# Gathering the second expert table by four tokens and two heads, and multiplying it in four 32-column groups

## The chip, the cores and the metric

The kernel runs on one core of a Trainium2 chip. The metric is the device time of one execution in microseconds (us): the median of 3 runs of the kernel before is 1951.93 us (1950.73 to 1953.85). Lower is better.

## The reference

One decoder layer over 512 tokens of width 1024: an attention part, a gated DeltaNet part, an output projection, and then a retrieval layer over 128 x 128 experts (PEER). Only the last one is touched:

```python
s1, s2 = query halves @ keys1, keys2           # 8 heads x 128 keys each, per token
v1, i1 = top_k(s1, 16); v2, i2 = top_k(s2, 16)
top_score, pos = top_k(v1[..., :, None] + v2[..., None, :], 16)
expert_id = (i1 * 128 + i2)[pos]; gate = softmax(top_score)
# per token 8 heads x 16 = 128 selections
act = gelu(einsum('tkd,td->tk', u_tab[expert_id], h))
y = einsum('tk,tkd->td', gate * act, v_tab[expert_id])
x = x + y
```

Each of the 512 tokens reads 128 rows of `peer_u` and 128 rows of `peer_v`, all of 1024 float32 (4 KB): 131,072 rows, 537 MB.

## The kernel before

Up to the output projection everything is unrolled; the PEER layer then works on 4 tiles of 128 tokens, one token in each partition. For a tile there are 128 steps c (head h = c // 16, rank k = c % 16). All of it meets in these steps:

- GpSimd (`gather`, L456 to L488) issues for each c one indirect DMA of 128 rows of `peer_u` (row p is the expert that token p chose as its selection c) into one of 8 buffers `u_row`, and one of `peer_v` into one of 8 buffers `v_row`. `peer_v` runs one head (16 steps) behind `peer_u`. In the first tile `peer_v` is held until head 2 and is then issued twice per step for 16 steps. Both kinds are in one instruction stream: a gather that waits for its buffer holds back those behind it.
- VectorE (`tile`, L1320 to L1360) waits for the u row and multiplies and sums it against h in one instruction (L1336), which frees the u buffer. After each head it waits for ScalarE's gelu and makes the weights `wt` (L1355). Between steps it also runs `choose` (L1273), the top-k of one head: in the first tile its own heads at c in `FIRST_AT`, and for the next tile the eight heads at c = 88, 93, ..., 123 (`NEXT_AT` and every 5). The next tile's ids go to `eid_n` and are copied into `eid` by `take` (L1313) when the gathers have read the old ones.
- ScalarE (`diagonal`, L945) turns each column of weights into a 128 x 128 diagonal matrix, in one of 8 buffers.
- TensorE (L763 to L791) multiplies the diagonal by the v row in two halves of 512 columns, which adds the weighted rows of 128 tokens to PSUM banks 6 and 7. After it the v buffer is free. Between these it computes the next tile's queries: half a query with every step from c = 36 to 67 (L736), then 16 score matmuls (L744) at c = 68.
- When a tile is done, ScalarE's `finish` copies the banks to `y_s`, and SyncE stores it.

The four tiles are written as tile 0, a hardware loop over tiles 1 and 2, and tile 3 (`tiles`, L281). Waits on buffers whose number depends on the loop go through `by_itself` (L276), which adds an increment of a semaphore behind the wait.

## Time and profile before

| | before |
|---|---|
| median of 3 runs | 1951.93 us |
| lowest, highest | 1950.73, 1953.85 us |
| the profiled execution, its span | 2155.2 us |
| granted TensorE clock, mean | 0.912 |
| bytes moved by the gathers (software queue) | 536.94 MB |
| DMA engines' share, whole span | 66.9% in the gathers |

Times of instructions come from one profiled execution. It is 203 us longer than the median. The first gather is issued 522.6 us into it, the last at 2140.1 us. In rows of a timeline the columns are start in us, length in us, engine, line, operation, and in brackets how long the engine was idle before it and for whom. "issue" means that nothing in the profile shows what it waited for. The diagram of 40 slices shows the PEER layer from slice 10 on:

```profile
PEclk9999999889896998888989877899998879999999
DMA  3212020142696898889999977999997889999997
```

### The profile page before, as it was taken

How to read it: one execution, taken by the hardware profiler on the slowest of the kernel's cores; microseconds unless marked ns; L12 is line 12 of the kernel's file. 1: busy time of each engine (PE TensorE's matmuls, PEld its weight loads, DVE VectorE, ACT ScalarE, POOL GpSimd, SP SyncE). 2: the span in 40 equal slices, each digit the busy share in tenths (PEclk: the TensorE clock that was granted, in tenths of full speed). 3: DMA queues.
4: the chain of work that ended last, by engine and by line, in shares of the span. 5: the costliest groups of instructions: out<-in, count | busy, mean ns of one | idle time of the engine just before them, and what ended most of it. 6: DMA issues, size and time to landing. Idle time of an engine off the chain costs nothing.

```text
span 2155.2 us, 19891 instructions
## 1 busy us (share of the span) xinstructions
PE 1638.5 (76%) x5306; PEld 838.8 (39%) x5306; DVE 1147.4 (53%) x2739; ACT 346.6 (16%) x780; POOL 1046.2 (49%) x1111
## 2 busy tenths in 40 slices
PE   5989989888782977567769765686895567676778
PEld 3445567767331543223236422232552222222223
DVE  3424446564857436884454477545436784444441
ACT  2331223221120111111111111211111111111111
POOL 3001012202463565566666555666665566666664
PEclk9999999889896998888989877899998879999999
DMA  3212020142696898889999977999997889999997
GB/s 119 78 39 79 0 78 1 40 147 94 247 359 239 330 346 314 294 303 364 379 345 337 336 276 288 359 378 349 351 350 297 301 301 365 374 375 348 366 368 290
DMA packets 161218, 571.36 MB, mean 265 GB/s; under 512 B 19152, under 2 KB 19152, under 8 KB 160080
## 3 DMA queue, kind: packets, MB, share of 16 engines
q0 software_dynamic: 147456, 536.94, 66.9%
q1 hardware_dynamic: 13648, 33.10, 4.3%
q8 instruction: 47, 0.77, 0.1%
q14 instruction: 67, 0.55, 0.1%
HBM read 567.87 MB, written 2.10 MB: 264 GB/s over the span
## 4 chain that ended last, share of the span: by engine, by line
PE 40%; issue 19%; DVE 18%; DMA 7%; POOL 7%; DVEq 5%; another core or an unknown queue 2%; ACT 1%; POOLq 1%; ACTq 0%
PE psum L788 15%; DVE arena L1336 7%; POOL arena L458 6%; PE psum L538 5%; PE psum L736 4%; PE psum L536 4%; DMA arena<-in_peer_u,arena 4%; DMA arena<-in_peer_v,arena 3%; DVE arena L1245 2%; PE psum L590 1%; DVE arena L1246 1%; PE psum L650 1%; DVE arena L1242 1%; DVE arena L1249 1%
## 5 line engine op out<-in xcount | busy, mean ns | idle before, releaser
L788 PE MATMUL psum<-arena 128*128 128x512 f32 x2048 | 1014.9, 634 | 352.8 <-DMA arena<-in_peer_v,arena 138.3
L1336 DVE CUSTOM_DVE_ANT_0 arena<-arena,psum 128x1024 f32<-128x1024 f32 x512 | 613.5, 1220 | 516.4 <-DMA arena<-in_peer_u,arena 413.9
L788 PEld LDWEIGHTS psum<-arena 128*128 128x128 f32 x2048 | 385.1, 201 | 910.9 <-issue 848.0
L458 POOL DMA_INDIRECT arena<-in_peer_u,arena x512 | 482.6, 943 | 381.6 <-issue 211.2
L458 POOL DMA_INDIRECT arena<-in_peer_v,arena x512 | 484.2, 946 | 340.0 <-issue 138.9
L948 ACT ACTIVATE arena<-ident,arena 128x128 f32<-128x128 f32 x512 | 175.5, 393 | 605.2 <-PE psum L788 328.1
L422 POOL TENSOR_TENSOR arena<-arena 128x512 f32<-128x512 f32 x28 | 37.1, 1335 | 249.2 <-DVE arena L1176 135.8
L736 PEld LDWEIGHTS psum<-arena 128*128 128x128 f32 x1024 | 132.4, 194 | 63.5 <-issue 63.5
L736 PE MATMUL psum<-arena 128*128 128x128 f32 x1024 | 135.3, 278 | 13.2 <-issue 11.7
L538 PE MATMUL psum<-arena 128*128 128x512 f32 x256 | 114.0, 592 | 0.0
L980 ACT ACTIVATE arena<-arena 128x16 f32<-128x16 f32 x32 | 6.9, 217 | 519.1 <-DVEq L1346 380.9
L536 PE MATMUL psum<-arena 128*128 128x512 f32 x192 | 86.5, 606 | 0.0
L538 PEld LDWEIGHTS psum<-arena 128*128 128x128 f32 x256 | 46.7, 190 | 49.3 <-issue 49.3
L713 PE MATMUL psum<-arena 128*128 128x512 f32 x128 | 57.3, 608 | 1.4 <-ACT arena L926 1.4
L436 POOL TENSOR_TENSOR arena<-arena,g_rs 128x512 f32<-128x512 f32 x8 | 9.1, 1174 | 99.0 <-DVEq L1119 99.0
L536 PEld LDWEIGHTS psum<-arena 128*128 128x128 f32 x192 | 36.7, 195 | 42.7 <-issue 42.4
L1249 DVE MAX8 arena<-arena 128x8 f32<-128x128 f32 (+1 forms) x96 | 29.3, 333 | 27.5 <-issue 23.8
L1336 DVE DVE_READ_ACCUMULATOR2_ANT arena<- 128x1 f32 x512 | 42.2, 82 | 0.0
L730 PE MATMUL psum<-ident,arena 128*128 128x128 f32 x32 | 6.9, 386 | 45.0 <-DVE arena L1266 45.0
L744 PE MATMUL psum<-arena 128*128 128x128 f32 x128 | 22.1, 350 | 24.0 <-ACT arena L937 17.7
L661 PE MATMUL psum<-arena 128*128 128x128 f32 x192 | 38.6, 296 | 0.0
L660 PE MATMUL psum<-arena 128*128 128x128 f32 x160 | 35.7, 308 | 3.8 <-ACT arena L909 3.7
(197 smaller groups left out, 1241.7 us busy)
## 6 DMA issues: line engine op xcount, KB each, us to landing
arena<-in_w_in SPq DMA_DIRECT2D x7, 2048.0 KB, 8.4
arena<-in_peer_w_q SPq DMA_DIRECT2D x8, 1024.0 KB, 5.9
arena<-in_peer_u,arena POOLq DMA_INDIRECT x512
arena<-in_peer_v,arena POOLq DMA_INDIRECT x512
arena<-in_w_out SPq DMA_DIRECT2D x8, 512.0 KB, 7.0
arena<-in_x SPq DMA_DIRECT2D x4, 512.0 KB, 4.7
out<-arena SPq DMA_DIRECT2D x4, 512.0 KB
arena<-in_norm_g SPq DMA_DIRECT2D x1, 512.0 KB, 4.1
```

What stands on the lines that cost most here:

```text
L422: pool.tensor_tensor(ATs[n % 2], AT, lv_mask[:, lv].unsqueeze(1).to_broadcast([P, GH, P]), ALU.mult).then_inc(s["ats_rdy"], 1)
L458: pool.indirect_dma_start(buf, None, table, bass.IndirectOffsetOnAxis(ap=eid[:, col:col + 1], axis=0)).then_inc(landed, 16)
L536: mm = pe.matmul(ps, w[:, dc, u * P:(u + 1) * P], hT[:, dc], start=dc == 0, stop=dc == DC - 1)
L538: mm = pe.matmul(ps, hT[:, dc, u * P:(u + 1) * P], w[:, dc], start=dc == 0, stop=dc == DC - 1)
L661: mm = pe.matmul(bank[6][:, c], XW[:, h], tt, start=True, stop=True)
L713: mm = pe.matmul(bank[wo_bank(n)], mixT[:, t, c], w_out_s[c][:, half * 512:(half + 1) * 512], start=c == 0, stop=c == DC - 1)
L736: mm = pe.matmul(bank[j // 4][:, (j % 4) * P:(j % 4 + 1) * P], w_q_s[c][:, j * HALF:(j + 1) * HALF], h2T[:, c], start=c == 0, stop=c == DC ...
L788: mm = pe.matmul(bank[6 + half], diag[c % VB], v_row[c % VB][:, half * 512:(half + 1) * 512], start=False, stop=c == SEL - 1, skip_group_c ...
L948: act.activation(diag[c % VB], ident[:], ACT.Copy, scale=wt[:, c:c + 1]).then_inc(s["diag_rdy"], 1)
L1245: dve.max_index(i_[:, 0:8], o[:, 0:8], v)
L1249: dve.max(o[:, 8:16], l_)
L1336: dve.tensor_tensor_reduce(u_row[c % UB], u_row[c % UB], h2p, 1.0, 0.0, ALU.mult, ALU.add, dots[:, c:c + 1]).then_inc(s["u_free"], 1)
```

## The change

It changes what one gather of `peer_v` holds. Before, it holds one selection of 128 tokens. Now it holds 32 selections (two heads, a "unit") of 4 tokens. The product with the weights then sums over the partitions, so that TensorE needs a 128 x 4 matrix of weights in place of a diagonal one. That matrix is 32 columns wide (28 of them zero), it writes 32 partitions of PSUM, and four gathers in a row go to the four groups of 32 columns. The parts:

- `choose` transposes the ids of each two heads in blocks of 32 x 32 on VectorE (`eidT`). `weigh` does so for the weights, and spreads them with one multiplication into `zrows` (two of them, in turn), where each gather's four columns stand in a window of 32. ScalarE's 512 diagonals are gone.
- TensorE's `rows` takes four gathers at a time: 8 matmuls, and one increment of `v_free` by 4 behind them. Buffers of v are freed four at a time. The number of matmuls and the columns that they stream are as before.
- `peer_v` runs a unit (32 steps) behind `peer_u`, never two to a step. After the last u gather, 32 v gathers are left, where 16 were.
- `eid` and `gates` have two buffers each; `take` is gone. The gelu is one for each unit (16 in all, not 32), and VectorE makes the weights one step into the next unit, so it doesn't wait for it on the spot.
- The tiles are written out, without the loop and without `by_itself`.
- Places: the next tile's chooses stand at c = 100, 103, ..., 121 in tile 0 and at 72, 77, ..., 107 in tiles 1 and 2 (before 88, 93, ..., 123 in all). The queries stand at c = 66 to 81, two halves a step, in tile 0, and at 22 to 53 in tiles 1 and 2; scores at 82 and 54.
- The result goes in place into `xs`, in an order of tokens that `swap` (a permuted identity) sets, and is stored with four DMAs a tile.

The diff, cut:

```diff
+UH = 2
+UK = UH * TOPK
+NQ = P // UK
+UNITS = NT * PH // UH
+ZG, ZW = 36, 32
...
-        FIRST_AT = [3, 22, 35, 38, 41, 44, 47]
+        FIRST_AT = [3, 19, 35, 38, 41, 44, 47]
...
+                self.norm = 47 if i == 0 else 15
+                self.turn = 2 * UK if i == 0 else 20
+                self.query = self.turn + 2
+                self.step = 2 if i == 0 else 1
+                self.score = self.query + 2 * NS // self.step
+                self.choose = 100 if i == 0 else 72
+                self.every = 3 if i == 0 else 5
...
+        def unit_rows(j):
+            group, place = j % NQ, j // NQ
+            return group, place, group * (UK // NQ) + place
...
-            with sp.Fori(0, NT) as i:
-                sp.wait_ge(s["y_out"], i + 2)
-                sp.dma_start(out_d[:, bass.ds(i, 1)].rearrange("p o d -> p (o d)"), y_s).then_inc(s["stored"], 16)
+            for i in range(NT):
+                sp.wait_ge(s["y_out"], i + 1)
+                for q in range(NQ):
+                    sp.dma_start(out_d[q * UK:(q + 1) * UK, i], xs[q::NQ, i]).then_inc(s["stored"], 16)
...
+            def gather_v(k, j):
+                n = k * UK + j
+                at_ = unit_rows(j)[2]
+                if j == 0:
+                    pool.wait_ge(s["eidT_rdy"], k + 1)
+                if n >= VB:
+                    pool.wait_ge(s["v_free"], n - VB + 1)
+                pool.indirect_dma_start(v_row[n % VB], None, v_d,
+                                        bass.IndirectOffsetOnAxis(ap=eidT[k % (2 * PH // UH)][:, at_:at_ + 1], axis=0)
+                                        ).then_inc(v_in[n % VB], 16)
...
+            for i in range(NT):
+                for c in range(SEL):
+                    k, j = divmod(i * SEL + c, UK)
+                    gather_u(i, c)
+                    if k == 1 and j == 0:
                         pool.wait_ge(s["wo_ps"], 2 * NT)
-                        if is_first(i) and h <= 2:
-
-                            if h == 2:
-                                gather_v(0, 2 * k)
-                                gather_v(0, 2 * k + 1)
-                        elif h >= 1:
-                            gather_v(i * SEL, (h - 1) * TOPK + k)
+                        pool.memset(zrows[0], 0.0)
+                        pool.memset(zrows[1], 0.0).then_inc(s["z_clear"], 1)
+                    if k >= 1:
+                        gather_v(k - 1, j)
+            for j in range(UK):
+                gather_v(UNITS - 1, j)
...
+                    pe.wait_ge(s["z_rdy"], k + 1)
+                last = k % (SEL // UK) == SEL // UK - 1 and j + NQ == UK
                 for half in range(2):
+                    for jj in range(j, j + NQ):
+                        n = k * UK + jj
+                        group, place, at_ = unit_rows(jj)
+                        z0 = at_ * ZG - place * (ZG - ZW)
+                        if half == 0:
+                            pe.wait_ge(v_in[n % VB], 16 * (n // VB + 1))
+                        mm = pe.matmul(bank[6 + half][group * UK:(group + 1) * UK],
+                                       zrows[k % 2][:, z0:z0 + ZW],
+                                       v_row[n % VB][:, half * 512:(half + 1) * 512],
+                                       start=False, stop=last, skip_group_check=True)
+                mm.then_inc(s["v_free"], NQ)
...
-                    pe.wait_ge(s["diag_rdy"], i * SEL + c + 1)
-                    pe.wait_ge(v_in[c % VB], 16 * (i * (SEL // VB) + c // VB + 1))
-                    for half in range(2):
-                        mm = pe.matmul(bank[6 + half], diag[c % VB], v_row[c % VB][:, half * 512:(half + 1) * 512],
-                                       start=False, stop=c == SEL - 1, skip_group_check=True)
-                    mm.then_inc(s["v_free"], 1)
...
-            def diagonal(row, c):
-                act.wait_ge(s["v_free"], SEL + row + c - VB + 1)
-                act.activation(diag[c % VB], ident[:], ACT.Copy, scale=wt[:, c:c + 1]).then_inc(s["diag_rdy"], 1)
...
+                if h % UH == UH - 1:
+                    k = (t * PH + h) // UH
+                    if k >= 2 * PH // UH:
+                        dve.wait_ge(s["v_free"], (k - 2 * PH // UH + 1) * UK)
+                    dve.drain()
+                    dve.transpose(eidT[k % (2 * PH // UH)], into_id[:, (h - UH + 1) * TOPK:(h + 1) * TOPK]).then_inc(s["eidT_rdy"], 1)
...
+            def weigh(k):
+                i = k * UK // SEL
+                c = slice(k * UK % SEL, k * UK % SEL + UK)
+                dve.wait_ge(s["gel_rdy"], k + 1)
+                dve.drain()
+                dve.tensor_tensor(wt[:, c], gel[:, c], gates[i % 2][:, c], ALU.mult)
+                dve.drain()
+                dve.transpose(wT, wt[:, c])
...
+                dve.drain()
+                dve.tensor_tensor(zrows[k % 2].rearrange("p (g x) -> p g x", x=ZG)[:, :, 0:NQ].rearrange("p (a b) x -> p a b x", a=NQ),
+                                  wT.rearrange("p (a b) -> p a b", a=NQ).unsqueeze(3).to_broadcast([P, NQ, UK // NQ, NQ]),
+                                  quarter.unsqueeze(1).unsqueeze(1).to_broadcast([P, NQ, UK // NQ, NQ]),
+                                  ALU.mult).then_inc(s["z_rdy"], 1)
...
+                    if c % UK == 1 and n >= UK:
+                        weigh(n // UK - 1)
+            weigh(UNITS - 1)
```

## Rows read from the trace of the kernel before

**Rows 1.** The page: the span, and busy time by engine (us, share, instructions).

```profile
span 2155.2 us, 19891 instructions
PE 1638.5 (76%) x5306; PEld 838.8 (39%) x5306; DVE 1147.4 (53%) x2739; ACT 346.6 (16%) x780; POOL 1046.2 (49%) x1111
```

**Rows 2.** Windows: stretch, length, each engine's busy us, granted clock, DMA share, GB/s.

```profile
600.00:700.00 100.00, 56.55 (x127) 22.83 (x126) 67.32 (x226) 9.83 (x26) 50.45 (x54) 0.83 0.79 293
700.00:800.00 100.00, 92.87 (x399) 56.13 (x398) 44.14 (x77) 14.87 (x40) 61.76 (x66) 0.99 0.91 332
800.00:950.00 150.00, 92.47 (x210) 40.13 (x209) 110.28 (x358) 20.32 (x50) 80.74 (x86) 0.84 0.84 309
1200.00:1350.00 150.00, 94.59 (x212) 42.85 (x211) 108.25 (x352) 18.32 (x48) 79.62 (x85) 0.79 0.81 295
1600.00:1750.00 150.00, 94.03 (x230) 40.90 (x229) 104.68 (x332) 18.12 (x47) 79.10 (x83) 0.85 0.80 293
1800.00:2100.00 300.00, 213.19 (x424) 74.62 (x423) 129.99 (x219) 40.71 (x120) 196.09 (x209) 0.97 0.96 368
```

**Rows 3.** The gathers' line L458: what ended GpSimd's idle time before them.

```profile
  DVE arena L1336: 168.3, 57
  PE psum L788: 156.4, 63
```

**Rows 4.** Timeline of GpSimd, tile 0; the second row is step c = 80.

```profile
772.74 0.94 POOL L458 DMA_INDIRECT arena<-in_peer_v,arena  x1 [3.35 <-remote]
773.99 0.94 POOL L458 DMA_INDIRECT arena<-in_peer_u,arena  x1 [0.30 <-DVE arena L1336]
```

**Rows 5.** Timeline of VectorE, tile 3: two u rows one after the other.

```profile
2107.79 1.22 DVE L1336 CUSTOM_DVE_ANT_0 arena<-arena,psum 128x1024 f32<-128x1024 f32 x1 [1.33 <-DMA arena<-in_peer_u,arena]
2110.35 1.22 DVE L1336 CUSTOM_DVE_ANT_0 arena<-arena,psum 128x1024 f32<-128x1024 f32 x1 [1.33 <-DMA arena<-in_peer_u,arena]
```

**Rows 6.** Timeline of VectorE: a choose from first to last instruction, then two u rows.

```profile
813.96 0.50 DVE L1242 MAX8 arena<-psum 128x8 f32<-128x128 f32 x2 [9.01 <-PE psum L744]
...
823.04 0.17 DVE L1297 SCALAR_TENSOR_TENSOR arena<-arena 128x16 uint32<-128x16 f32 x1
823.22 1.22 DVE L1336 CUSTOM_DVE_ANT_0 arena<-arena,psum 128x1024 f32<-128x1024 f32 x1
...
824.37 1.22 DVE L1336 CUSTOM_DVE_ANT_0 arena<-arena,psum 128x1024 f32<-128x1024 f32 x1
```

**Rows 7.** Timeline of VectorE: first and last instruction of a later choose.

```profile
644.67 0.50 DVE L1242 MAX8 arena<-psum 128x8 f32<-128x128 f32 x2
...
662.17 0.18 DVE L1297 SCALAR_TENSOR_TENSOR arena<-arena 128x16 uint32<-128x16 f32 x1
```

**Rows 8.** Timeline of GpSimd: step 32 of tile 0, the first v rows behind it.

```profile
585.75 0.94 POOL L458 DMA_INDIRECT arena<-in_peer_u,arena  x1 [1.11 <-issue]
587.00 0.94 POOL L458 DMA_INDIRECT arena<-in_peer_v,arena  x1 [0.30 <-DVE arena L1336]
```

**Rows 9.** Timeline: the last u gather, the last gelu, the last products.

```profile
2110.68 0.94 POOL L458 DMA_INDIRECT arena<-in_peer_u,arena  x1 [0.30 <-issue]
...
2119.73 0.21 ACT L980 ACTIVATE arena<-arena 128x16 f32<-128x16 f32 x1 [15.26 <-DVEq L1346]
...
2126.63 24.27 PE L788 MATMUL psum<-arena 128*128 128x512 f32 x56 [0.56 <-issue]
```

**Rows 10.** Timeline of TensorE: one step's query half, one v row; tile 0's scores.

```profile
798.07 1.05 PE L736 MATMUL psum<-arena 128*128 128x128 f32 x8
...
798.96 1.88 PE L788 MATMUL psum<-arena 128*128 128x512 f32 x4
...
808.25 5.52 PE L744 MATMUL psum<-arena 128*128 128x128 f32 x32 [7.42 <-ACT arena L937]
```

**Rows 11.** Timeline of VectorE: a head's end inside the choose stretch of tile 0.

```profile
899.65 0.08 DVE L1336 DVE_READ_ACCUMULATOR2_ANT arena<- 128x1 f32 x1
900.29 0.18 DVE L1355 TENSOR_TENSOR arena<-arena 128x16 f32<-128x16 f32 x1 [0.56 <-ACT arena L980]
```

More of the change, by code:

```diff
@@ L486, in _, with gather_u @@
-            pool.wait_ge(s["mixT_ps"], NT)
-            tiles(pool, tile)
-            for k in range(TOPK):
-                gather_v((NT - 1) * SEL, (PH - 1) * TOPK + k)
+            def gather_u(i, c):
+                n = i * SEL + c
+                if c % TOPK == 0:
+                    pool.wait_ge(s["eid_rdy"], i * PH + c // TOPK + 1)
+                if n >= UB:
+                    pool.wait_ge(s["u_free"], n - UB + 1)
+                pool.indirect_dma_start(u_row[n % UB], None, u_d, bass.IndirectOffsetOnAxis(ap=eid[i % 2][:, c:c + 1], axis=0)
+                                        ).then_inc(u_in[n % UB], 16)
@@ L771, in tile @@
+            for i in range(NT):
                 for c in range(SEL):
-                    if not is_last(i):
-                        if c == TURN_AT:
+                    w = PLACES[i]
+                    if i + 1 < NT:
+                        if c == w.turn:
                             pe.wait_ge(s["picked"], (i + 1) * PH)
                             turn_h2(i + 1)
-                        if QUERY_AT <= c < SCORE_AT:
-                            if c == QUERY_AT:
+                        if w.query <= c < w.score:
+                            if c == w.query:
@@ L779, in tile @@
                                 pe.wait_ge(s["h2T_out"], i + 2)
-                            mm = query((c - QUERY_AT) // 2, (c - QUERY_AT) % 2, 2)
-                            if c == SCORE_AT - 1:
+                            for x in range((c - w.query) * w.step, (c - w.query + 1) * w.step):
+                                mm = query(x // 2, x % 2, 2)
+                            if c == w.score - 1:
                                 mm.then_inc(s["q_ps"], 1)
-                        if c == SCORE_AT:
+                        if c == w.score:
@@ L795, in _ @@
+                    if k >= 1 and j % NQ == 0:
+                        rows(k - 1, j)
+            for j in range(0, UK, NQ):
+                rows(UNITS - 1, j)
         @block.scalar
@@ L966, in load_h2, with gelu @@
                 ins.then_inc(s["h2p_rdy"], 1)
+            def gelu(k):
+                c = slice(k % (SEL // UK) * UK, (k % (SEL // UK) + 1) * UK)
+                act.wait_ge(s["dots_rdy"], k + 1)
+                act.activation(gel[:, c], dots[:, c], ACT.Gelu).then_inc(s["gel_rdy"], 1)
             turned_h2(0)
@@ L1255, in norm2 @@
             def norm2(t):
-                xt = x2[:, bass.ds(t * D, D)]
-                if not is_first(t):
-                    by_itself(dve, s["h2T_ps"], t)
+                xt = xs[:, t]
+                if t:
+                    dve.wait_ge(s["h2T_ps"], t)
                 dve.drain()
@@ L1362, in _ @@
-            tiles(dve, tile)
+                choose(0, h, h == EARLY - 1)
+            soften(0, gates[0], 0, EARLY)
+            for i in range(NT):
+                dve.wait_ge(s["h2p_rdy"], i + 1)
+                for c in range(SEL):
+                    n = i * SEL + c
+                    if i == 0 and c in RESIDUAL_AT:
+                        residual(3 + RESIDUAL_AT.index(c))
+                    dve.wait_ge(u_in[n % UB], 16 * (n // UB + 1))
+                    dve.tensor_tensor_reduce(u_row[n % UB], u_row[n % UB], h2p, 1.0, 0.0, ALU.mult, ALU.add,
+                                             dots[:, c:c + 1]).then_inc(s["u_free"], 1)
+                    if c % UK == UK - 1:
+                        dve.drain()
+                        dve.engine_nop().then_inc(s["dots_rdy"], 1)
+                    if c == PLACES[i].norm and i + 1 < NT:
+                        norm2(i + 1)
+                    if chosen_after(i, c):
+                        who, head = chosen_after(i, c)
+                        last = head in ([PH - 1] if who else [h1 - 1 for _, h1, _ in GROUPS0])
+                        choose(i + who, head, last)
+                    for group, (h0, h1, after) in enumerate(GROUPS0):
+                        if i == 0 and c == after:
+                            soften(group, gates[0], h0, h1)
+                    if i >= 1 and c == SOFTEN_AT:
+                        soften(len(GROUPS0) + i - 1, gates[i % 2], 0, PH)
+                    if c % UK == 1 and n >= UK:
+                        weigh(n // UK - 1)
```

220 lines of the change are left out of this document (77 added, 143 removed).

## The prediction

> **What bounds the kernel now.** I read the busy times first, then the layer in windows, then what ends the waits of the gathers, and last the timelines from which the prices come. The totals show no full engine: VectorE is busy 53% and GpSimd 49% of a span of 2155.2 us [rows 1]. The windows tell more. In tile 3, where nothing but rows is worked on, the DMA engines are at a share of 0.96 and move 368 GB/s [rows 2]: transfers are the bound there. In the three stretches in which the next tile's heads are chosen the share falls to 0.84, 0.81 and 0.80, while VectorE is busy 110, 108 and 105 of 150 us [rows 2]: there VectorE is the bound. In the stretch with the queries TensorE is busy 93 of 100 us, and the share is 0.91 [rows 2]: there TensorE takes part. The waits of the gathers say the same twice: 168 us until VectorE has freed a u buffer, 156 us until TensorE has freed a v buffer [rows 3]. Part of this is harmless, since GpSimd issues a gather every 1.25 us (773.99 less 772.74) [rows 4], and the transfers are slower than that: two u rows, between which lie two gathers, follow each other by 2.56 us (2110.35 less 2107.79) [rows 5], 1.28 us a gather. At that pace 1024 gathers take 1311 us.
>
> The number of gathers, their bytes and the streamed columns of TensorE stay. So the change can only win or lose the time in which the transfers stand still. Over the six windows of rows 2 that is, with (1 less share) by length, 21, 9, 24, 29, 30 and 12 us.
>
> **Profile and median.** The profiled execution is 203 us longer than the median, and no row tells in which stretch. I sum changes against the span of 2155.2 us and carry the sum to the median unscaled, since its terms are made of VectorE's and TensorE's instruction times and of the 2.56 us a pair, the quickest steady pace seen.
>
> **The places of the chooses.** One choose takes 9.26 us from its first to its last instruction (823.22 less 813.96), and a u row costs 1.15 us of VectorE when rows are waiting (824.37 less 823.22) [rows 6]. From c = 88 to 128, tile 0 needs VectorE before for 40 x 1.15 + 8 x 9.26 = 120 us, against 40 x 2.56 = 102 us of transfers. After, c = 88 to 100 goes at the transfers' pace (12 x 2.56 = 31 us), then 28 x 1.15 + 74 = 106 us on VectorE: 137 us. The denser places cost 17 us in tile 0. Some chooses take longer in the profile (17.7 us, 644.67 to 662.35, with gaps that nothing explains) [rows 7]. The difference of the two cases does not depend on it, since both have eight of them. In tiles 1 and 2 the spacing is 5 as before: 0.
>
> **What VectorE no longer waits for.** A head's end costs it 0.8 us inside such a stretch (899.65 to the weights at 900.29, and 0.18 for them) [rows 11], three times a stretch, and `take`, its wait, and the switch to the next tile fall into it too, some 2 us. In tiles 1 and 2 the stretch now ends at c = 107, and there is one `weigh` in it. I give the new transposes and `weigh` 1.5 us a unit, worked out as a handful of small instructions like the 0.18 us one of rows 11 with their drains. The trace has none of them: bounds 0.5 and 4 us a unit. Gain about 3 us in each of the three stretches: 9 us less, bounds 0 and 15.
>
> **The v gathers that come later.** Before, 16 v gathers are fitted in two behind each u gather, at c = 32 to 47 of tile 0, from 587.0 on [rows 8]. There VectorE has five chooses and 16 rows, 5 x 9.26 + 16 x 1.15 = 65 us, and 48 gathers need 61 us: they were nearly free. After, only 32 are there, 41 us, and the transfers stand. The 16 lie at the end. There before, from the issue of the last u gather at 2110.7 [rows 9] to the end of the span 44.5 us pass: the last gelu at 2119.7, the last 14 v rows on TensorE in 24.27 us (56 records, four a row) [rows 9], 1.73 us each, then copies and the store. After: gelu as before, weights 2 us later, a first group of four rows, then 24 gathers at 1.28 to 1.44 us (31 to 35), the last group, copies, four stores: some 58 us if the four column groups run side by side, and 9 + 2 + 32 x 1.73 + 5 = 71 us if they don't. That is 13 to 27 us more. The early part gives 5 us back: step 35, and with it the row of chooses that bounds this part, comes sooner when one gather goes with each step and not two. Sum 8 to 22 us, 10 taken with side by side.
>
> **TensorE.** An undisturbed v row costs 1.88 us, half a query 1.05, the scores 5.5 us and before them 7.4 us of waiting for ScalarE's copy [rows 10]. Before, a step with a query costs 2.9 us against 2.56: over 32 steps 12 us behind, then 13 us for the scores. Eight v buffers cover 8 x 2.56 = 20 us of it, so some 5 us a tile are lost, 15 in all. After, four steps cost 4.2 us of queries and the rows of a group, which lies between 1.9 (all side by side) and 7.5 us (none), against 10.2. In tiles 1 and 2 that is no loss in most of this range. In tile 0 the queries come two halves a step: 8.4 us and the rows, 10.3 to 15.9, against 10.2, over four groups, and then the scores. The loss stays there. Gain 10 us; with no overlap of the groups 0, and even a loss of 3.
>
> What shows TensorE's speed is the granted clock: 0.97 in tile 3 and 0.79 to 0.85 where it starves between rows [rows 2], between full speed (2.4 GHz) and half (1.2 GHz). Catching up after such a stretch gets cheaper with groups: 4 us less.
>
> **Buffers freed in fours.** The worst gather of v must now wait until the group five rows back is done, not until one row eight back is. When it waits, four v and about five u gathers are still under way: 9 x 1.28 = 11.5 us of transfers. TensorE's work behind the last landed row of a group is at most five rows' halves at 0.94, 4.7 us at full clock and 9.4 at half; issue and first data take another 3 us (I take the 2.56 us of rows 5 and round up). It fits but for half the clock. 0, bounds 0 and 15 us.
>
> **Removed at no gain.** The 512 diagonals lie beside the gathers' bound. The increments behind the waits lie beside as well: step 80 begins a head and so has two waits with increments ahead of its gather, and the gap before it is 0.30 us [rows 4], the same as elsewhere. The loop's end likewise. The two memsets on GpSimd (some 2 us, ahead of the first v gather; everything behind them in its queue waits) lie in a part that VectorE bounds.
>
> **The sum.** +17 - 9 + 10 - 10 - 4 = +4 with the groups fully side by side. With none it is +17 - 9 + 22 + 3 = +33. The pairs of records of one float32 matmul go to the same columns one behind the other, so I expect half the overlap, and take +14: 2169 us of span, 1966 us of median.
>
> The Trainium skill, "TensorE: Matmul & The Clock Gate" (Part 3, packing small matmuls), gives a speedup of 2.38 for three column tiles of 32 with 512 columns, and says that matmuls keep their order in start and end. No row here shows a column tile. By it the sum would lie at the lower end, near +6.
>
> **The rivals.**
> *TensorE holds the gathers, and the change frees them.* For it: 156 us of waits for v buffers [rows 3], 92.87 of 100 us busy [rows 2]. Against it: where TensorE is fullest the transfers lose only 9 us in 100. If the median runs, with quicker transfers than the profile, are held by TensorE in the query and catching-up stretches, then 3 x (9 + 5) = 42 us come from there (the 9 us of that window and 5 us of lag, for each of three tiles). With the 9 us of VectorE and less the 17 of tile 0 that is 34 less: 1918 to 1940. Chance 0.28.
> *Nothing moves.* Transfers are the bound, and gains and losses cancel within 4 us: 1952. For it speaks the sum for full overlap. The skill's "DMA: Bandwidth & Descriptors" (Specifications) puts a core's share of HBM at about 358 GB/s, by which the layer would be bound by transfers wherever it is placed. Tile 3 moves 368 GB/s over 300 us [rows 2], above it. Chance 0.12.
> *The groups don't overlap and come late.* This ends slower by more: the worst case of the sum, 33, and half a clock in the gaps between groups, which makes up to 15 us: 1985 to 2000. It decides when the rows of a group take over 8.5 us behind the last landing (11.5 less 3). Chance 0.15.
> *The forecast*, 1958 to 1983: 0.45. If the new instructions ask for another order of time altogether (a store by rows of four partitions, say), that is outside all of these.
>
> **How the numbers follow.** The likeliest is 1966. Faster cases hold 0.28, so the range reaches down to 1925, and up to 2005 with most of the third case. A measurement of this kernel tells 0.2%, 4 us, from no change. Slower by more than that: 0.45 + 0.15 = 0.60, within 0.12, faster 0.28.
>
> **What would show it.** In the profile after: in c = 100 to 127 of tile 0 the DMA share under 0.7 with VectorE nearly full, and waits on L1336 there. From the last u gather to the end 55 to 70 us, not 44.5. Shares of 0.95 or more where the queries are in tiles 1 and 2. If groups overlap, the products' busy time falls well under 1000 us. Waits for TensorE's v buffers under 100 us say that the relief is real. I'm wrong if tile 0 and the tail are longer by less than 15 us together, or if tile 3 alone gets quicker or slower than 2.56 to 2.9 us a pair.

## The result, and the profile after

The changed kernel takes 1972.88 us (median of 4 runs, 1967.81 to 1975.73) against 1951.33 us for the kernel before on the same chip: a ratio of 1.0111, interval 1.0089 to 1.0134. It is 21.6 us slower, where 14 us slower was forecast.

Chips differ. On some, here called quick, the kernel before takes about 1951 us; on others, called slow, 2124 to 2156. (Three chips were slow, and the one of c3, e6b and e7 was quick; that of this first comparison isn't on record. No chip was met twice, so it isn't shown that a chip always keeps its pace.) The trace that the prediction read is from a slow one, and the trace of after from a quick one. So the rows of before that answer to it are those of a later run of the kernel before on a quick chip (c3_before_third, below), and ratios are always of two kernels on one chip. Where rows 1 have a span of 2155.2 us and rows 3 waits of 168.3 and 156.4 us, the page and the view of the gathers' line of before say this on a quick chip:

```profile
span 1955.1 us, 19891 instructions
PE 1601.5 (82%) x5306; PEld 822.5 (42%) x5306; DVE 1148.1 (59%) x2739; ACT 353.1 (18%) x780; POOL 1042.3 (53%) x1111
DMA  3121120014279899999999999999999999999997
L458 POOL DMA_INDIRECT arena<-in_peer_u,arena x512: 932/937/1548, 525.4 to 1903.5; - x171
  DVE arena L1336: 106.8, 109
  PE psum L788: 85.9, 124
```

And after (L475 is now the u gather, L486 the v gather, L795 the product, L1313 the copy that ends a choose):

```profile
span 1966.0 us, 16121 instructions
PE 1378.3 (70%) x5306; PEld 548.1 (28%) x5306; DVE 1151.7 (59%) x2765; ACT 166.8 (8%) x250; POOL 1047.4 (53%) x1116
DMA  3121120023379799979999979999997999999998
L795 PE MATMUL psum<-arena 128*32 128x512 f32 x2048 | 754.2, 825 | 507.3 <-DMA arena<-in_peer_v,arena 416.7
L475 POOL DMA_INDIRECT arena<-in_peer_u,arena x512: 932/937/1835, 516.8 to 1898.9; - x171
  DVE arena L1365: 125.9, 100
L486 POOL DMA_INDIRECT arena<-in_peer_v,arena x512: 932/937/1843, 579.8 to 1952.9; - x171
  PE psum L795: 74.9, 54
DMA to landing us min/median/max: 4.9/9.0/11.8
```

The diagrams of 40 slices, counted from 0, tell a part. On a quick chip before has 9s from slice 14 to the last but one; after has 7s between them, in the stretches in which the next tile's heads are chosen (slices 17, 23, 30), as at 13, where the first tile's own are. But a 9 is 90% or anything above. The page's row of GB/s, of before and then of after, shows that before's choose stretches fall too, to between 334 and 375 (slices 17, 23 to 25, 30 to 32), only less deep than after's:

```profile
GB/s 131 54 76 43 44 86 1 1 49 156 68 278 394 316 396 396 380 334 372 410 409 407 390 375 336 351 410 409 408 409 373 351 337 410 409 410 409 409 409 282
GB/s 130 53 76 43 44 86 1 6 81 118 129 278 356 261 409 409 339 249 366 410 409 409 398 288 410 410 409 409 409 401 282 410 409 409 410 410 409 409 376 297
```

TensorE lost 223 us of busy time and ScalarE half of its own, and the span is no shorter. From the first u gather to the end it is 1955.1 less 525.4 = 1429.7 us before and 1966.0 less 516.8 = 1449.2 after: 19.5 us longer. (The part ahead of it varies by several us between runs of one program and isn't touched.)

Windows on quick chips show where. Before: steps 32 to 63, 64 to 95 and 96 to 127 of tile 0 by the issues of their u gathers, then tile 3, then from the last u gather on (stretch, length, busy of PE, PEld, DVE, ACT, POOL, clock, DMA share, GB/s):

```profile
584.00:699.00 115.00, 86.76 (x226) 38.99 (x227) 90.26 (x269) 21.77 (x54) 75.42 (x80) 0.90 0.91 354
699.00:783.00 84.00, 83.76 (x374) 51.86 (x373) 44.52 (x99) 13.51 (x35) 59.68 (x64) 1.00 1.02 400
783.00:880.00 97.00, 68.78 (x144) 27.95 (x142) 88.72 (x282) 12.63 (x34) 60.71 (x66) 0.88 0.95 357
1582.00:1903.00 321.00, 241.61 (x493) 86.17 (x494) 165.06 (x301) 50.83 (x143) 237.74 (x254) 0.98 1.02 404
1903.00:1955.00 52.00, 42.68 (x96) 17.28 (x94) 8.78 (x15) 6.94 (x19) 16.95 (x19) 1.00 0.75 290
```

After, the same stretches:

```profile
574.00:684.00 110.00, 54.59 (x127) 8.60 (x125) 92.33 (x276) 3.06 (x4) 62.91 (x66) 0.71 0.81 298
684.00:764.00 80.00, 66.60 (x420) 39.25 (x421) 37.98 (x66) 3.11 (x3) 59.67 (x64) 0.89 1.03 409
764.00:876.00 112.00, 66.69 (x140) 8.83 (x135) 93.95 (x311) 1.51 (x2) 60.28 (x65) 0.64 0.85 316
1571.00:1899.00 328.00, 209.01 (x511) 30.38 (x508) 159.66 (x269) 4.38 (x9) 238.34 (x256) 0.75 1.03 409
1899.00:1966.00 67.00, 46.94 (x154) 7.96 (x154) 5.61 (x11) 1.30 (x3) 31.68 (x34) 0.91 0.82 303
```

Counted by the u rows as VectorE takes them up (the starts of the instruction that the prediction has at L1336, now L1365): steps 0 to 63 of tile 0 are 7.3 us shorter (177.9 to 170.6), 64 to 87 the same, 88 to 127 12.4 longer (127.7 to 140.1: the dense chooses), tile 1 is 12.5 shorter (353.1 to 340.6), tile 2 2.8 shorter, tile 3 6.2 longer, and from the last u row to the end 35.0 us have become 58.1. Together +19.5. Tiles 2 and 3 belong together: before leaves tile 2 with VectorE behind and catches up in tile 3 (its first 16 u rows there take 35.9 us, and 16 rows of the steady part 41.0 in both kernels).

### The profile page after: what moved, and what is told of

Read it like the earlier page. It is cut to its first block, busy times and chain, and to the rows that moved or that the text cites. A ratio compares the mean times of both kernels' runs of the same rounds, so it can differ in the third digit from the quotient of the medians.

```text
span 1966.0 us, 16121 instructions
## 1 busy us (share of the span) xinstructions
PE 1378.3 (70%) x5306; PEld 548.1 (28%) x5306; DVE 1151.7 (59%) x2765; ACT 166.8 (8%) x250; POOL 1047.4 (53%) x1116
## 4 chain that ended last, share of the span: by engine, by line
PE 25%; DVE 23%; DMA 20%; POOL 17%; issue 9%; DVEq 4%; ACT 1%; POOLq 0%; ACTq 0%
DMA arena<-in_peer_u,arena 11%; DVE arena L1365 10%; DMA arena<-in_peer_v,arena 9%; POOL arena L486 8%; POOL arena L475 8%; PE psum L551 6%; PE psum L549 4%; PE psum L795 3%; DVE arena L1260 2%; PE psum L726 2%; PE psum L603 2%; DVE arena L1261 1%; PE psum L663 1%; DVE arena L1257 1%; DVE arena L1264 1%
## 5 line engine op out<-in xcount | busy, mean ns | idle before, releaser
L795 PE MATMUL psum<-arena 128*32 128x512 f32 x2048 | 754.2, 825 | 507.3 <-DMA arena<-in_peer_v,arena 416.7
L1365 DVE CUSTOM_DVE_ANT_0 arena<-arena,psum 128x1024 f32<-128x1024 f32 x512 | 613.8, 1218 | 439.5 <-DMA arena<-in_peer_u,arena 437.8
L475 POOL DMA_INDIRECT arena<-in_peer_u,arena x512 | 482.4, 942 | 322.0 <-DVE arena L1365 125.9
L486 POOL DMA_INDIRECT arena<-in_peer_v,arena x512 | 482.0, 941 | 217.0 <-issue 141.0
L795 PEld LDWEIGHTS psum<-arena 128*32 128x32 f32 x2048 | 113.2, 127 | 1122.7 <-DMA arena<-in_peer_v,arena 875.7
L749 PEld LDWEIGHTS psum<-arena 128*128 128x128 f32 x1024 | 117.3, 193 | 25.6 <-issue 25.6
L749 PE MATMUL psum<-arena 128*128 128x128 f32 x1024 | 121.9, 279 | 1.2 <-ACT arena L962 1.2
L551 PE MATMUL psum<-arena 128*128 128x512 f32 x256 | 114.0, 592 | 0.0
L549 PE MATMUL psum<-arena 128*128 128x512 f32 x192 | 85.8, 602 | 0.0
L726 PE MATMUL psum<-arena 128*128 128x512 f32 x128 | 63.3, 656 | 9.2 <-DVE arena L1244 7.7
L551 PEld LDWEIGHTS psum<-arena 128*128 128x128 f32 x256 | 46.7, 190 | 49.3 <-issue 49.3
L549 PEld LDWEIGHTS psum<-arena 128*128 128x128 f32 x192 | 36.3, 193 | 42.2 <-issue 42.0
L1365 DVE DVE_READ_ACCUMULATOR2_ANT arena<- 128x1 f32 x512 | 42.2, 83 | 0.0
L726 PEld LDWEIGHTS psum<-arena 128*128 128x128 f32 x128 | 26.5, 211 | 44.0 <-issue 44.0
L674 PE MATMUL psum<-arena 128*128 128x128 f32 x192 | 37.6, 289 | 0.0
L1084 DVE TENSOR_SCALAR arena<-arena,cwc 128x512 f32<-128x512 f32 x12 | 6.7, 561 | 52.3 <-ACT arena L865 52.1
L673 PE MATMUL psum<-arena 128*128 128x128 f32 x160 | 34.6, 301 | 3.9 <-ACT arena L938 3.7
L663 PE MATMUL psum<-arena 128*128 128x128 f32 x192 | 26.4, 280 | 8.6 <-DVE arena L1222 6.1
```

The source lines that it names most:

```text
L475: pool.indirect_dma_start(u_row[n % UB], None, u_d, bass.IndirectOffsetOnAxis(ap=eid[i % 2][:, c:c + 1], axis=0)).then_inc(u_in[n % UB], 16)
L486: pool.indirect_dma_start(v_row[n % VB], None, v_d, bass.IndirectOffsetOnAxis(ap=eidT[k % (2 * PH // UH)][:, at_:at_ + 1], axis=0)).then_i ...
L549: mm = pe.matmul(ps, w[:, dc, u * P:(u + 1) * P], hT[:, dc], start=dc == 0, stop=dc == DC - 1)
L551: mm = pe.matmul(ps, hT[:, dc, u * P:(u + 1) * P], w[:, dc], start=dc == 0, stop=dc == DC - 1)
L663: mm = pe.matmul(bank[4][:, h * P:(h + 1) * P], ATs[n % 2][:, h], TI[:, h] if i else ident[:], start=True, stop=True)
L726: mm = pe.matmul(bank[wo_bank(n)], mixT[:, t, c], w_out_s[c][:, half * 512:(half + 1) * 512], start=c == 0, stop=c == DC - 1)
```

## Experiments

All spaced kernels change constants of the list of places alone. They were made to say which part of the change costs what, in the changed kernel.

**The kernel before again**, unchanged, one execution.

> The kernel before, unchanged, for a second trace. The profile of the kernel after has a span of 1966.0 us, that is its own measured time, its gathers follow each other at 1.28 us and every choose takes 9.2 to 9.6 us. The first profile of before has a span of 2155.2 us, 203 us over its median, a pair of gathers every 2.8 us in tile 3 and chooses of up to 21 us. Theory: that one execution was a disturbed one, and a second trace shows a span of 1945 to 1960 us, 2.56 us a pair in tile 3 and chooses of 9.3 us. Rival: the kernel before is slowed whenever it is profiled (its hardware loop or its many small instructions), and the span is again 2100 us or more.

2123.72 us, on a slow chip, where eleven other executions of the kernel before took 2127 to 2143 us. So the 203 us between the first trace and the median are no cost of the profile.

**The chooses of tile 0 at their old spacing.**

```diff
-                self.choose = 100 if i == 0 else 72
-                self.every = 3 if i == 0 else 5
+                self.choose = 88 if i == 0 else 72
+                self.every = 5
```

> The kernel after with the chooses of tile 0 at c = 88, 93, ..., 123 in place of 100, 103, ..., 121, as the kernel before has them. Theory (the prediction's first term): the dense places cost 12 x (2.56 - 1.15) = 17 us, so this runs 17 us (12 to 20) faster than after's 1972.9, near 1956. Rival 1: eight buffers of u rows cover the lag in both, and it is within 4 us of after. Rival 2: a wait of the unit's weights behind the lagging chooses (the products of a new unit start at c = 97) takes back half of it, gain 5 to 10 us.

0.9875 (0.9847 to 0.9902) of before on a slow chip.

**The chooses of tiles 1 and 2 over more steps.**

```diff
-                self.choose = 100 if i == 0 else 72
-                self.every = 3 if i == 0 else 5
+                self.choose = 100 if i == 0 else 60
+                self.every = 3 if i == 0 else 8
```

> The kernel after with the chooses of tiles 1 and 2 at c = 60, 68, ..., 116 in place of 72, 77, ..., 107. In the trace of after, c = 64 to 111 takes 141 us in tile 1 where a stretch without chooses takes 123, so 18 us are lost in each. With a choose in every 8 steps VectorE needs 8 x 1.15 + 9.3 = 18.5 us against 20.5 us of transfers and never falls behind. Theory: both losses go, 30 to 36 us faster than after, near 1940, and faster than before. Rival: the transfers stand for another reason there (v buffers freed in fours, the scores on TensorE), and it is within 6 us of after.

0.9816 (0.9786 to 0.9845), slow chip.

**Both.** `self.choose = 88 if i == 0 else 60`, `self.every = 5 if i == 0 else 8`.

> The places of both: tile 0 at 88 and every 5, tiles 1 and 2 at 60 and every 8. Theory: the gains add, 45 to 55 us faster than after, near 1923, 1.5% faster than before. Rival: the gains overlap, since one slack covers both, and it is no faster than the better of the two by over 5 us.

0.9754 (0.9726 to 0.9782), slow chip.

**The changed kernel again**, since the three before it had run on another chip than it, and **the kernel before again**.

> The kernel after, unchanged. The job before this one ran on a chip on which the kernel before takes 2136 us, not 1951, and a pair of gathers 2.8 us, not 2.56. On such a chip the transfers leave VectorE more time in the choose stretches. If the gains of the two changes of places add, after took 2107.6 + 2095.4 - 2082.7 = 2120 us there, 0.993 of before. Theory: on a slow chip after is at 0.990 to 0.997 of before, on a quick one (before at 1951) at 1.011 again. Rival: the change costs the same everywhere, and the ratio is 1.008 or more on a slow chip too; then the two changes of places did not add, and each was worth over 40 us.

> The kernel before, unchanged, for its trace. On a quick chip: span near 1950, 2.56 us a pair, chooses of 9.3 us, and from the last u gather to the end 40 to 45 us. On a slow one the trace of the first job again (2122, 2.8 us a pair).

The changed kernel was 0.9963 (0.9942 to 0.9983) of before on a slow chip; the kernel before 2132.9 us there. The sign of the whole change depends on the chip. From these two on there is a base on slow chips, 0.9963 x 2134 = 2126 us, and against it e2 gains 0.0088 (19 us), e3 0.0147 (31 us) and e4 0.0209 (45 us; a few us less than the sum of its parts). Base and spaced kernels ran on two different slow chips, and the intervals of the two ratios leave each of these gains some 7 us either way. What lies in the transfers is to be seen in the diagrams of slices. The changed kernel on a slow chip:

```profile
DMA  3212020141776998789999879999987899999998
```

and with both spaced:

```profile
DMA  3212020131776898999999899999999999999997
```

The 7s and 8s from slice 15 on (15 to 17, 22 and 23, 29 to 31) are the choose stretches. They fill up, but for an 8 at 15 and at 22, when a choose comes every 8 steps: 8 x 2.56 = 20.5 us of transfers against 9.3 + 8 x 1.15 = 18.5 us of VectorE (rows 5 and 6), where 5 steps give 12.8 against 15.0. In tile 0 a spacing of 5 doesn't fill them either, but its steps 88 to 127 take 137.8 us of u rows in e2 against 152.4 in the changed kernel on a slow chip, 15 us less.

**Row by row: the overlap of groups and the freeing in fours taken away together.** Each row's two halves follow each other, as before, and each row frees its buffer.

```diff
-                for half in range(2):
-                    for jj in range(j, j + NQ):
+                for jj in range(j, j + NQ):
+                    for half in range(2):
...
-                mm.then_inc(s["v_free"], NQ)
+                    mm.then_inc(s["v_free"], 1)
```

> The kernel after, but each v row's two halves are multiplied one behind the other and its buffer is freed at once, not four rows by four. So the groups no longer run side by side, and TensorE needs 1.73 us a row again, as before the change. Theory (transfers and VectorE are the bound, not TensorE; the prediction's terms for the overlap were 4 to 13 us): within 6 us of after in the main part, and the last 32 rows at 1.73 us in place of some 1.5, 5 to 8 us more; together 0 to 12 us slower than after. Rival: freeing in fours is what costs, and this is 10 us or more faster than after. Second rival: the overlap carries the kernel, and this is 25 us or more slower.

0.9961 (0.9938 to 0.9984) on a slow chip, beside 0.9963 of the changed kernel. The product's group in the page, of this kernel and then of the changed one, both on slow chips:

```profile
L795 PE MATMUL psum<-arena 128*32 128x512 f32 x2048 | 856.4, 670 | 466.6 <-DMA arena<-in_peer_v,arena 304.7
```

```profile
L795 PE MATMUL psum<-arena 128*32 128x512 f32 x2048 | 775.6, 850 | 591.9 <-DMA arena<-in_peer_v,arena 429.8
```

TensorE is 81 us longer busy and the time is the same. On a slow chip the overlap and the freeing in fours together change nothing that can be measured; that a gain of the one and a cost of the other cancel isn't ruled out, since they were taken away together. That busy time differs by no more than 81 us has in part to do with the clock: the mean granted clock is 0.90 in this kernel and 0.80 in the changed one. The view of L795 gives the shortest, median and longest of its records in ns, of this kernel and then of the changed one; the median is at full clock in the one and at half in the other:

```profile
L795 PE MATMUL psum<-arena x2048: 589/592/1063, 595.2 to 2126.9; 128*32 128x512 f32 x187
L795 PE MATMUL psum<-arena x2048: 589/1018/1063, 591.1 to 2110.5; 128*32 128x512 f32 x187
```

A second run of it was on another slow chip:

> The kernel after with the rows multiplied one by one and each buffer freed at once, a second time, for a quick chip (before near 1951), where the transfers leave TensorE less time: a row costs it 1.73 us, half a query 1.06, against 2.56 us a pair. Theory (VectorE and the transfers are the bound, and TensorE's relief is worth little): 1.006 to 1.016 of before, as after's 1.011. Rival: on a quick chip the overlap carries something, since the kernel before waits 10 us a tile for v buffers around its queries there: 1.017 to 1.025. On a slow chip: 0.996 again.

0.993 (0.991 to 0.995), a little under the 0.996 that was expected for a slow chip. For quick chips this stays open.

**The first tile's own chooses spaced too**, on top of both:

```diff
-        FIRST_AT = [3, 19, 35, 38, 41, 44, 47]
+        FIRST_AT = [3, 19, 35, 40, 45, 50, 55]
...
-                self.norm = 47 if i == 0 else 15
+                self.norm = 57 if i == 0 else 15
```

> The version with all chooses spaced (tile 0 at 88 and every 5, tiles 1 and 2 at 60 and every 8) and besides the first tile's own chooses at c = 35, 40, 45, 50, 55 in place of 35, 38, 41, 44, 47, its norm at 57. In the trace of after, c = 32 to 63 takes 110 us where 82 are needed. Theory: VectorE's lag there falls from 60 - 31 = 29 to 69 - 51 = 18 us, 8 to 12 us faster than the spaced version (on the slow chip near 2073 us, on a quick one near 1912). Rival: the lag is bounded by the step at which the turned norm is ready (c = 64), and it is within 4 us of the spaced version or slower.

0.9665 (0.9633 to 0.9697) on a slow chip. That is 2064.0 us against 2126.3 of the changed kernel on the same chip, 62 us less, and 0.0089 (19 us) under both spaced, where 8 to 12 were expected. In the traces it is 18 us from the first to the last u gather (1491.1 to 1472.8), only 9 of them before step 64 of tile 0.

**The kernel before a third time, the same spaced kernel again, and one with more buffers at the end.** These three ran on one quick chip.

> The kernel before, unchanged, for its trace, in the hope of a quick chip (before near 1951). There: span near 1950, 2.56 us a pair, chooses of 9.3 us, the choose stretch of tile 0 (c = 96 to 127) slower than in tile 3 by some 20 us where after's is slower by 30, and 40 to 45 us from the last u gather to the end where after has 67. On a slow chip: the trace of the other jobs again.

1956.85 us; its rows are above.

> The version with all chooses spaced, a second time. On a slow chip: 0.967 of before again. On a quick one, where after is at 1.011: the transfers leave VectorE less time there, so the spacing is worth more, 22 + 17 + 2 x 18 + 10 = 60 us or more less than after: 1.011 less 0.031 to 0.036, 0.975 to 0.980. Rival: what is worth 62 us on a slow chip is worth half of it on a quick one, where a choose never takes over 9.6 us, and the ratio is 0.99 or more.

0.9804 (0.979 to 0.9817), 1912.9 us against 1952.65. That is 0.0307 under the changed kernel on a quick chip, 60 us: nearly as much as on a slow one, and about the least that was expected. Steps 64 to 127 of tile 1 show the place. Before, the changed kernel, and spaced:

```profile
1048.00:1232.00 184.00, 154.23 (x526) 81.09 (x525) 133.90 (x377) 26.24 (x69) 120.33 (x128) 0.94 0.97 372
```

```profile
1045.00:1226.00 181.00, 98.64 (x258) 15.05 (x258) 143.77 (x420) 2.05 (x4) 120.94 (x129) 0.72 0.96 374
```

```profile
1011.00:1179.00 168.00, 104.04 (x266) 15.63 (x259) 142.98 (x419) 2.05 (x4) 120.94 (x129) 0.73 1.03 409
```

For the same 64 steps and the same 143 us of VectorE, 181 us at 374 GB/s have become 168 at 409.

For the last kernel nothing but the tail changes: the last 32 v gathers go in turn into the 8 v buffers and the 8 u buffers, which by then are read for the last time.

```diff
+        def v_place(n):
+            if n < LAST:
+                return v_row[n % VB], v_in[n % VB], 16 * (n // VB + 1)
+            turn, b = divmod(n - LAST, 2 * VB)
+            if b < VB:
+                return v_row[b], v_in[b], 16 * (LAST // VB + turn + 1)
+            return u_row[b - VB], u_in[b - VB], 16 * (NT * SEL // UB + turn + 1)
```

> The version with all chooses spaced, and the last unit's 32 v rows go to 16 buffers, the 8 of v and the 8 of u, which are free by then. In the trace of after, the last u gather is issued 67 us before the end; the 9th v gather of the last unit waits 5 us for the weights, and from there 24 gathers take 40 us, 1.66 us each with a wait of 2.3 us in every eight, against 1.28 a gather. Theory: the tail is dear because v buffers are freed four at a time and only once the last weights are there; with 16 buffers it takes 5 to 12 us less, and so does the kernel. Rival: the landing of the transfers bounds the tail, and it is within 2 us of the version without.

0.9783 (0.9769 to 0.9797), 1909.06 us: 3.8 us less than the kernel without it, between the two expectations, with intervals that overlap a little. The traces show more clearly that the tail is shorter. From the last u gather to the end (e6b, then this one) it is 68 and 63 us:

```profile
1841.00:1909.00 68.00, 47.74 (x154) 8.12 (x154) 5.78 (x13) 1.30 (x3) 31.83 (x34) 0.90 0.82 297
```

```profile
1849.00:1912.00 63.00, 45.69 (x154) 7.97 (x154) 6.23 (x13) 1.30 (x3) 32.17 (x35) 0.91 0.83 320
```

So buffers are some 4 to 5 us of the tail. This version beats both kernels: 2.2% under before.

## Why the prediction was right or wrong

The sign and the range held, and the size was off by 8 us. But the 14 us came out of a sum of +4 and 10 us added for an overlap that was expected to be half there. The reason given for the 10 us was wrong, and the tail and the reliefs were both off the other way. That the forecast lies within 8 us of the result is in part luck.

**The dense chooses of tile 0: right.** +17 summed, less the 3 us that VectorE was to win in the same steps, makes +14; the traces of quick chips have +12.4, and on slow chips spacing them alone gives 19 us back (e2), 15 of them in these steps. There the change as a whole costs only 4.5 us in them (147.9 to 152.4), so something else in it wins some 10 us back; what it is wasn't looked for. The marker was half right: VectorE is nearly full there (93.95 of 112 us), but the share of the stretch is 0.85 (0.83 from c = 100 on), not under 0.7.

**The early part, -5: right on a quick chip**, with 7.3 us. On a slow chip the view of the gathers' line shows how much more it can be, before and then after:

```profile
L458 POOL DMA_INDIRECT arena<-in_peer_u,arena x512: 932/937/1659, 519.4 to 2090.3; - x171
```

```profile
L475 POOL DMA_INDIRECT arena<-in_peer_u,arena x512: 932/937/1663, 516.7 to 2050.2; - x171
```

From the first to the last u gather the change gains 37 us there (1570.9 to 1533.5; 21 us of it before step 64 of tile 0, 21 in tile 1, by u rows) and then loses 25 (to the end of the span 40.9 against 66.3 us). On a quick chip the first difference is 1378.1 to 1382.1, 4 us lost. In this part the sign differs between the chips. What the change wins there on a slow chip, and not on a quick one, stays open; e5, whose median there is the changed kernel's within 3 us, speaks against the groups side by side. (The changed kernel's execution in the trace is 8 us below its median, so the 37 us are rather too many.) Here was a fault of method: the terms were read from a trace of a slow chip and the sum was carried "unscaled" to a median of quick ones.

**The tail, +13 with groups side by side: mis-sized, at +15.5 or +23.** Counted from the last u gather's issue, as the prediction did, the level was 58 us and is 67.1, and before took 51.6 and not 44.5 on this chip, which makes +15.5. Counted from the last u row on VectorE, which counts the rows already on their way with their own stretch, it is +23.1 (and +22 on a slow chip). The two counts differ because VectorE takes up the last u row 16.7 us after its gather in before and 9.0 us after it in after. By the first count all that lies ahead of the tail is +4.0, by the second -3.6, and the sum had -11 for it; so by the prediction's own count the larger miss lies ahead of the tail. (Its early part and tail, -5 and +13, also make 8, where 10 stood in the sum.) Timeline of after:

```profile
1898.86 0.94 POOL L475 DMA_INDIRECT arena<-in_peer_u,arena  x1 [0.31 <-issue]
1900.10 0.94 POOL L486 DMA_INDIRECT arena<-in_peer_v,arena  x1 [0.30 <-issue]
1909.12 6.90 PE L795 MATMUL psum<-arena 128*32 128x512 f32 x26 [0.86 <-DMA arena<-in_peer_v,arena]
1910.11 0.29 DVE L1346 TENSOR_TENSOR arena<-arena,st 128x128 f32<-128x128 f32 x1
1913.02 0.94 POOL L486 DMA_INDIRECT arena<-in_peer_v,arena  x1 [4.96 <-PE psum L795]
1924.98 0.94 POOL L486 DMA_INDIRECT arena<-in_peer_v,arena  x1 [2.34 <-PE psum L795]
1940.04 2.33 PE L795 MATMUL psum<-arena 128*32 128x512 f32 x12 [0.21 <-DMA arena<-in_peer_v,arena]
1952.94 0.93 POOL L486 DMA_INDIRECT arena<-in_peer_v,arena  x1 [0.30 <-issue]
1958.75 1.90 PE L795 MATMUL psum<-arena 128*32 128x512 f32 x10 [0.19 <-DMA arena<-in_peer_v,arena]
```

The weights come 11 us after the last u gather, as forecast (9 + 2). The gathers of v don't. The prediction let eight of the last unit's 32 go ahead of them and summed 24. Only four do (1903.4 to 1907.1): the other four buffers hold the last rows of the unit before, whose last gather is issued at 1900.10 and lands 9.0 us later (1909.12), against the 3 us that the prediction took for issue and first data. The fifth waits 4.96 us for that. TensorE is at half clock when that row lands, after it has waited between the rows before: the granted clock is 0.50, the lower of its two levels, 1.2 GHz (the first number behind the busy times below), and the group is done 3.6 us after the landing (to 1912.74), where the last group of all, at full clock, takes 1.90.

```profile
1909.10:1912.90 3.80, 3.78 (x15) 0.89 (x15) 0.70 (x3) 0.23 (x1) 0.00 (x0) 0.50 0.72 280
```

From the fifth to the last, 28 gathers are issued over 39.9 us, 1.48 apart, with a wait of 2.3 us every eighth, where 31 to 35 us stood in the sum. (The expectation of e7 has 24 gathers at 1.66 us from the ninth on; the rows give 28 from the fifth on.) And the landing of the last one (5.8 us, to 1958.75) wasn't in the sum as a term. With twice the buffers (e7) the same 28 are issued over 33.6 us (1863.66 to 1897.22), at GpSimd's own pace of 1.24 us, but their last landing takes 7.9 us and not 5.8. That is the 4 to 5 us by which e7's tail is shorter:

```profile
1863.66 0.94 POOL L502 DMA_INDIRECT arena<-in_peer_v,arena  x1 [4.90 <-PE psum L812]
1897.22 0.94 POOL L502 DMA_INDIRECT arena<-in_peer_v,arena  x1 [0.30 <-issue]
1905.07 1.90 PE L812 MATMUL psum<-arena 128*32 128x512 f32 x10 [0.18 <-DMA arena<-in_peer_v,arena]
```

**Overlap of the column groups: wholly there in the engine, in part in the kernel.** The reason given for half the overlap, that the two records of one float32 matmul go to the same columns, doesn't hold them up: the 12 records at 1940.04 take 2.33 us in all, where 12 one behind the other take 5.2 (rows 9: 56 in 24.27 us). Four records of the four groups start within 0.02 us of each other (1940.04, .05, .06, .06), and each lasts 0.62 us. But a row's first half is multiplied when the row lands, and in the tail rows land one by one: of the 16 records of a group, four run alone (1.05 us a row) ahead of these 12. So a group takes about 4.4 us of TensorE, between the prediction's 1.9 (all side by side) and 7.5 (none). Besides, the clock is lower: 0.75 in tile 3, against 0.98 before. The marker, a product's busy time well under 1000 us, came out at 754 against 986.8, 24% less. The Trainium skill's rule by which the sum was near +6 ("TensorE: Matmul & The Clock Gate", Part 3: 2.38 for three column tiles) agrees with the direction, and where four rows are there four tiles went further here: four records in the time of one. That the +6 was 15 us too low is for the most part the work of the tail and of the reliefs.

**TensorE's relief, VectorE's and the catching up, -10, -9 and -4: the mechanism is there, the size is not.** Everything ahead of the tail was forecast at +17 - 5 - 9 - 10 - 4 = -11 and came out at -3.6 by u rows, +4.0 by u gathers. Of that, -20 was forecast outside of the early part and the chooses of tile 0 (-6, -10, -4), and -9 measured (0.2 - 12.5 - 2.8 + 6.2). The three can't be told apart further with these runs. What the trace does show is a new coupling, which the prediction had no term for. When VectorE is behind at a unit's end, in a choose stretch, the weights of 32 rows are late together (tile 1 of after):

```profile
1162.29 0.21 DVE L1319 STREAM_TRANSPOSE arena<-arena 128x32 uint32<-128x32 uint32 x1
1163.14 0.29 DVE L1346 TENSOR_TENSOR arena<-arena,st 128x128 f32<-128x128 f32 x1
1163.49 4.98 PE L795 MATMUL psum<-arena 128*32 128x512 f32 x32 [22.82 <-DVE arena L1346]
1167.07 0.94 POOL L486 DMA_INDIRECT arena<-in_peer_v,arena  x1 [10.37 <-PE psum L795]
```

TensorE stands for 22.8 us, and then the gather of v, and with it all gathers behind it, for 10.4. How much of the time is due to this coupling no run tells, since the spacing removes VectorE's lag and the coupling together. In this stretch (the three windows of tile 1 above) the changed kernel took 181 us, before 184 and the spaced one 168. The work of `weigh` is 0.76 us a unit (1162.59 to 1163.35) and that of the transposed ids 0.3 (1162.29 to 1162.59), together 1.1 and not 1.5. Where the queries stand the share is 1.03, in tiles 1 and 2 as forecast (c = 22 to 53), and in tile 0 as well (the second stretch of after), where the prediction left the loss: steps 64 to 95 take 80.5 us there and 84.5 before, by u gathers. The marker "waits for v buffers under 100 us" told nothing, since before itself has 85.9 us on a quick chip.

**Buffers freed in fours: 0, nothing against it where it was tried.** Row by row and in fours agree on a slow chip (0.9961 and 0.9963), with the overlap taken away as well. In the tail the freeing in fours shows as the 2.3 us waits, but nothing shows them to be a price: row by row the last 28 gathers are issued over 40.0 us (2079.13 to 2119.11), in fours over 40.5 (2062.19 to 2102.65), both on that chip.

**Removed at no gain: right.** ScalarE has 186 us less to do, GpSimd's own busy time stays, and the pace of tile 3 is 2.56 us a pair (128 in 328 us), within the 2.56 to 2.9 of the marker; before takes 321 us, since it catches up at the tile's start. The other sign of being wrong, tile 0 and the tail longer by less than 15 us together, didn't come either: they are 28 us longer by u rows.

**The rivals.** *TensorE holds the gathers, and the change frees them* is ruled out by the outcome: with 223 us less of TensorE's time the kernel is 21.6 us slower, not 12 to 34 faster. On a slow chip 81 us more (e5) moved nothing either; on a quick one that wasn't tried. *The groups don't overlap and come late* is ruled out by the four that start together. *Nothing moves* was near for all that lies ahead of the tail (-3.6 or +4.0 us); the tail decided. Transfers bound tile 3 at 409 GB/s, above the Trainium skill's 358 GB/s ("DMA: Bandwidth & Descriptors", Specifications), as the trace of a slow chip had it too (rows 2: 368).

## What to carry to other kernels

Where a stream of transfers is the bound, price a change by the stretches in which the stream stands, and by its two ends: here 223 us less TensorE time didn't shorten the kernel, 16 gathers moved from an early gap to the end made the tail 15 to 23 us longer, and constants that say where VectorE's top-k stands were worth 60. Of a tail, sum the landing of its last transfer and the time from issue to landing under load against the buffers, not the steady pace. And before a sum from one profile is carried to a median, find out whether both are of the same chip.

## What the runs showed of the hardware

- The chips met differ by 9 to 10% for this kernel: 1951 us against 2124 to 2156. In the steady stretch a quick chip moves 404 to 409 GB/s (1.28 us for a gather of 128 rows of 4 KB), a slow one 374, in one and the same changed kernel:

```profile
1782.00:2009.00 227.00, 137.98 (x324) 20.69 (x324) 100.56 (x170) 1.76 (x5) 150.32 (x162) 0.72 0.97 374
```

- The "17.7 us choose with gaps that nothing explains" (rows 7) comes with the slow chips: on quick ones each of the 32 takes 9.2 to 9.6 us.
- Four column groups of 32 run side by side with float32 and 512 columns when their rows are there (four records within 0.62 us and 0.02); TensorE's busy time fell by 14%, 1601 to 1378 us.
- Twice as many buffers in the last stretch moved the bound from the freeing of buffers (1.48 us a gather) to GpSimd's issue (1.24 us).
- A TensorE clock of 0.75 (after, tile 3) instead of 0.98 (before) didn't change the steady pace there, 41.0 us for 16 u rows in both: the products wait for gathers. At 0.50, where GpSimd waited for one group in the tail, that group took 3.6 us behind the last landing, against 1.90 at full clock.
